# Up products of the MLP and FFN loops as one 512-column product per weight tile, on an input rescaled once by GpSimd

## The reference, cut to what matters

```python
h = rmsnorm(x, norm_mlp_pre)               # first block
u = jnp.square(jax.nn.relu(h @ w_up))
x = x + rmsnorm(u @ w_down, norm_mlp_post)

# second block, layers a and b: h = rmsnorm(x, ffn_norm); up = h @ ffn_w_up  (2 x 2816 wide)
# causal 3-tap convolution over tokens with bias, silu of one half times the other, @ ffn_w_down
```

## Time and profile before

| | |
|---|---|
| median of 3 runs | 1091.08 us |
| profiled execution | 1091.15 us, span 1089.2 us |
| PE (TensorE matmul) busy | 1081.0 us, 99% of the span |
| DVE busy | 773.9 us, 71% |
| ACT busy | 641.3 us, 59% |
| POOL busy | 21.5 us, 2% |
| DMA | 183.90 MB, mean 169 GB/s |
| TensorE clock granted | 1.00 over the whole span |

### The profile page before, as it was taken

One profiled execution on the slowest core, in us unless ns is written; L12 is line 12 of the kernel. 1 busy time (PEld: TensorE's weight loads), 2 busy tenths in 40 slices (PEclk: granted clock), 3 DMA queues, 4 the chain that ended last, 5 costly groups with the idle time before them and its releaser, 6 DMA issues.

```text
span 1089.2 us, 19347 instructions
## 1 busy us (share of the span) xinstructions
PE 1081.0 (99%) x7132; PEld 946.2 (87%) x7132; DVE 773.9 (71%) x1389; ACT 641.3 (59%) x1104; POOL 21.5 (2%) x47
## 2 busy tenths in 40 slices
PE   9999999999999999999999999999999999999998
PEld 8977899998988887888888999999877789999997
DVE  5877765555567767666755877878876757787876
ACT  5477665445566657566566655555766756555553
POOL 0000000000000000000010000000001010000000
PEclk9999999999999999999999999999999999999999
DMA  8642456555646563365524565565563435656562
GB/s 314 184 143 98 147 183 200 187 184 184 194 125 211 165 197 114 101 196 187 163 72 154 164 205 187 161 211 179 169 193 103 150 116 170 198 173 211 170 197 97
DMA packets 117038, 183.90 MB, mean 169 GB/s; under 512 B 6640, under 2 KB 70384, under 8 KB 116720
## 3 DMA queue, kind: packets, MB, share of 16 engines
q1 hardware_dynamic: 116688, 182.77, 52.7%
q10 hardware_dynamic: 288, 0.29, 0.1%
HBM read 181.99 MB, written 1.05 MB: 168 GB/s over the span
## 4 chain that ended last, share of the span: by engine, by line
PE 89%; DVE 6%; ACT 3%; issue 1%; DMA 1%; SPq 0%; DVEq 0%; ACTq 0%
PE ps L687 11%; PE ps L689 10%; PE ps L688 10%; PE ps L715 9%; PE ps L717 9%; PE ps L716 9%; PE ps L777 5%; PE ps L776 5%; PE ps L778 5%; DVE w_lo L1857 3%; PE ps L878 2%; PE ps L855 1%; PE ps L908 1%; PE ps L951 1%; DVE hid L2363 1%; ACT w_hi L1263 1%
## 5 line engine op out<-in xcount | busy, mean ns | idle before, releaser
L1857 DVE TENSOR_TENSOR w_lo<-w_stage,w_hi 128x1024 fp32r<-128x1024 f32 x336 | 403.8, 1222 | 169.9 <-ACT w_hi L1263 169.0
L1263 ACT ACTIVATE w_hi<-w_stage 128x1024 fp32r<-128x1024 f32 x336 | 349.5, 1054 | 175.8 <-PE ps L689 81.7
L715 PE MATMUL ps<-aT_hi,w_hi 128*128 128x256 f32 x992 | 281.8, 284 | 0.6 <-issue 0.4
L716 PE MATMUL ps<-aT_lo,w_hi 128*128 128x256 f32 x992 | 281.1, 283 | 0.0
L717 PE MATMUL ps<-aT_hi,w_lo 128*128 128x256 f32 x992 | 281.1, 283 | 0.0
L687 PE MATMUL ps<-w_hi,aT_hi 128*128 128x512 f32 x480 | 192.8, 402 | 1.4 <-DVE w_lo L1932 0.9
L715 PEld LDWEIGHTS ps<-aT_hi,w_hi 128*128 128x128 f32 x992 | 190.5, 192 | 2.3 <-DVE w_lo L1857 0.7
L716 PEld LDWEIGHTS ps<-aT_lo,w_hi 128*128 128x128 f32 x992 | 190.5, 192 | 1.0
L717 PEld LDWEIGHTS ps<-aT_hi,w_lo 128*128 128x128 f32 x992 | 190.5, 192 | 0.0
L689 PE MATMUL ps<-w_hi,aT_lo 128*128 128x512 f32 x480 | 187.7, 391 | 0.0
L688 PE MATMUL ps<-w_lo,aT_hi 128*128 128x512 f32 x480 | 187.2, 390 | 0.0
(11 more groups left out here) (248 smaller groups left out, 1112.0 us busy)
## 6 DMA issues: line engine op xcount, KB each, us to landing
w_stage<-in_ffn_w_up SPq DMA_DIRECT2D x88, 512.0 KB, 4.7
w_stage<-in_a_w_qkv SPq DMA_DIRECT2D x72, 512.0 KB, 4.3
w_stage<-in_ffn_w_down SPq DMA_DIRECT2D x44, 512.0 KB, 3.5
w_stage<-in_w_up SPq DMA_DIRECT2D x32, 512.0 KB, 3.9
w_stage<-in_w_down SPq DMA_DIRECT2D x32, 512.0 KB, 4.3
w_stage<-in_w_in SPq DMA_DIRECT2D x24, 512.0 KB, 4.6
w_stage<-in_b_w_qkv SPq DMA_DIRECT2D x24, 512.0 KB, 4.0
w_stage<-in_w_out SPq DMA_DIRECT2D x8, 512.0 KB, 3.5
```

Of the source, the lines that this page charges most:

```text
L715: pe.matmul(o, wh, aT_hi[:, k, :], start=(k == 0), stop=False)
L716: pe.matmul(o, wh, aT_lo[:, k, :], start=False, stop=False)
L1263: act.activation(w_hi[:, slot, :], w_in[:, slot, :], ACT.Copy).then_inc(hi_done[slot], 1)
L1857: dve.tensor_tensor(w_lo[:, slot, :], w_in[:, slot, :], w_hi[:, slot, :].bitcast(F32), ALU.subtract).then_inc(lo_done[slot], 1)
```

## The change

In the MLP loop, the FFN loops and the FFN tails, the product of `w_hi` with `aT_hi` and that of `w_hi` with `aT_lo` become one product of 512 columns, whose halves go to the two halves of the PSUM bank. The third product (`w_lo` with the high part, 256 columns) adds into the first half. DVE adds the halves (`tensor_reduce` over two). As the scale can't be applied in that reduction, the input for these stages is scaled first: in each head GpSimd forms (hi + lo) times `rbc` for each of the 8 input tiles into one of two buffers (`pts`), ACT rounds it into `oT_hi` (`whole_hi`), GpSimd subtracts for `oT_lo`. TensorE waits for all 8 before the loop. The heads themselves keep the old products and scaling. In the MLP loop, relu and square become one DVE instruction (max(h, 0)·h), and ACT no longer squares.

```diff
-        oT_hi = sb("oT_hi", [P, KT, S], F32R)
-        oT_lo = sb("oT_lo", [P, KT, S], F32R)
+        oT_both = sb("oT_both", [P, 2, KT, S], F32R)
+        oT_hi, oT_lo = oT_both[:, 0], oT_both[:, 1]
...
@@ dense_cols
+                            if joined:
+                                both = ps[:, bank(stg, names[f]), :].rearrange("p (c s) -> p c s", c=2)
+                                if k == 0:
+                                    pe.matmul(both, wh, oT_both[:, :, k, :], start=True, stop=False)
+                                last = pe.matmul(o, wl, oT_hi[:, k, :], start=False, stop=False, skip_group_check=True)
+                                if k > 0:
+                                    last = pe.matmul(both, wh, oT_both[:, :, k, :], start=False, stop=(k == KT - 1))
...
@@ TensorE, MLP (each FFN likewise, both halves of its loop and its tail joined)
             down(S_, 0, 8, range(4), True, hidden_tiles(S_, 1, 0))
+            pe.wait_ge(s["whole_lo"], at(S_, "whole_lo", KT))
             S_ = st["mlp_loop"]
             with trips(pe, S_) as i:
-                dense_cols(S_, i, 0, A4)
+                dense_cols(S_, i, 0, A4, joined=True)
                 down(S_, i, 4, range(4), ready=hidden_tiles(S_, -3, i))
...
@@ ACT
+            def whole_hi(stg, ks):
+                for k in ks:
+                    act.wait_ge(s["whole"], at(stg, "whole", k + 1))
+                    act.activation(oT_hi[:, k, :], pts[:, k % 2, 0:S], ACT.Copy).then_inc(s["whole_hi"], 1)
...
             for f in range(4):
                 hidden_hi(S_, 0, f + 1, f * S)
-            square_up(S_, 0, 4, 1, B4)
+            whole_hi(S_, range(2))
+            square_up(S_, 0, 4, 1, B4, lambda pair: whole_hi(S_, range(2 + 2 * pair, 4 + 2 * pair)))
             for f in range(4):
                 split(S_, 8 + f)
                 hidden_hi(S_, 0, 4 + f + 1, f * S)
+                if f < 2:
+                    whole_hi(S_, [6 + f])
             S_ = st["mlp_loop"]
             with trips(act, S_) as i:
-                square_up(S_, i, 0, 0, A4)
+                splits(S_, range(4), i)
...
@@ ACT, FFN head
                 hidden_hi(S_, 0, 1, 0, W)
+                whole_hi(S_, range(2))
                 splits(S_, range(4, 6))
                 taps(S_, 0, B4, 1, (0, 1))
+                whole_hi(S_, range(2, 4))
                 splits(S_, range(6, 8))
                 gate(S_, 0, 2)
                 taps(S_, 0, B4, 1, (2, 3))
+                whole_hi(S_, range(4, 6))
                 splits(S_, range(8, 10))
+                whole_hi(S_, range(6, 8))
                 hidden_hi(S_, 0, 2, 0, W)
...
@@ GpSimd, once for each of the three heads
+            def whole_input(stg, scale):
+                chain.enter(stg, 0)
+                pool.wait_ge(*is_drained(scale, "scale"))
+                def low(k):
+                    pool.wait_ge(s["whole_hi"], at(stg, "whole_hi", k + 1))
+                    pool.tensor_tensor(oT_lo[:, k, :], pts[:, k % 2, 0:S], oT_hi[:, k, :].bitcast(F32),
+                                       ALU.subtract).then_inc(s["whole_lo"], 1)
+                for k in range(KT):
+                    t = pts[:, k % 2, 0:S]
+                    if k >= 2:
+                        low(k - 2)
+                        pool.wait_ge(s["whole_lo"], at(stg, "whole_lo", k - 1))
+                    chain.link(pool.tensor_tensor(t, aT_hi[:, k, :].bitcast(F32), aT_lo[:, k, :].bitcast(F32), ALU.add))
+                    pool.tensor_tensor(t, t, rbc[:], ALU.mult).then_inc(s["whole"], 1)
+                low(KT - 2)
+                low(KT - 1)
...
@@ DVE, MLP loop
+            def square_up(stg, i, n0, names):
+                for pair in range(2):
+                    split(stg, n0 + 2 * pair, i)
+                    for f in (2 * pair, 2 * pair + 1):
+                        dve.wait_ge(*is_full(stg, names[f], i))
+                        dve.tensor_reduce(hid[:, f, :], ps[:, 4 + f, :].rearrange("p (c s) -> p s c", c=2), AX.X, ALU.add)\
+                            .then_inc(drained[4 + f], 1)
+                        dve.wait_ge(*is_drained(stg, names[f], i))
+                        dve.wait_ge(s["uhi"], at(stg, "uhi", f - 3, i))
+                        dve.scalar_tensor_tensor(out=u32[:, f * S:(f + 1) * S], in0=hid[:, f, :], scalar=0.0,
+                                                 in1=hid[:, f, :], op0=ALU.max, op1=ALU.mult).then_inc(s["u"], 1)
+                    split(stg, n0 + 2 * pair + 1, i)
...
@@ DVE, FFN loops and tails: scale_up becomes
+                def join_up(stg, i, names, fs):
+                    for f in fs:
+                        dve.wait_ge(*is_full(stg, names[f], i))
+                        dve.tensor_reduce(scaled[:, f, :], ps[:, 4 + f, :].rearrange("p (c s) -> p s c", c=2), AX.X, ALU.add)\
+                            .then_inc(drained[4 + f], 1)
```

More of the change, by code:

```diff
@@ L281, in make_plan @@
     acc = [(f"acc{b}", b) for b in range(4)]
+    whole = {"pool_step": 8, "whole": 8, "whole_hi": 8, "whole_lo": 8}
     def ffn(tag):
@@ L288, in ffn @@
                   quarters=up_quarters("a", BY_DEPTH) + up_quarters("b") + [None] * 2,
-                  counts={k: 2 * v for k, v in up.items()}),
+                  counts={**{k: 2 * v for k, v in up.items()}, **whole}),
             Stage(f"ffn_{tag}_loop", trips=(U2 - 3) // 2, uses=up_names("a") + up_names("b"),
@@ L305, in make_plan @@
         Stage("mlp_head", uses=up_names("a") + up_names("b"),
-              quarters=up_quarters("a") + up_quarters("b") + [None] * 4, counts={k: 2 * v for k, v in mlp_up.items()}),
+              quarters=up_quarters("a") + up_quarters("b") + [None] * 4,
+              counts={**{k: 2 * v for k, v in mlp_up.items()}, **whole}),
         Stage("mlp_loop", trips=U1 - 2, uses=up_names("a"), quarters=up_quarters("a") + [None] * 4, counts=mlp_up),
@@ L445, in blocks_kernel @@
             "orstd", "osq", "hms", "dm", "ovar", "sig", "sq", "ms8", "rs8", "silu", "u", "uhi", "ulo", "msq", "pms", "prstd", "x_new",
-            "lam", "zeroed", "const_ready", "gate_w", "unit", "rd", "rdb", "bc", "ohi", "olo")}
+            "lam", "pool_step", "whole", "whole_hi", "whole_lo", "zeroed", "const_ready", "gate_w", "unit", "rd", "rdb", "bc", "ohi", "olo")}
         def is_full(stg, name, i=0):
@@ L697, in dense_rows, with dense_cols @@
                         after[q]()
-            def dense_cols(stg, i, n0, names, turned=None, after=None, order=BY_PAIRS, each=None):
+            def dense_cols(stg, i, n0, names, turned=None, after=None, order=BY_PAIRS, each=None,
+                           joined=False):
                 for q, (pair, deep) in enumerate(order):
@@ L714, in dense_cols @@
                                 pe.wait_ge(*is_free(stg, names[f], i))
-                            pe.matmul(o, wh, aT_hi[:, k, :], start=(k == 0), stop=False)
-                            pe.matmul(o, wh, aT_lo[:, k, :], start=False, stop=False)
-                            last = pe.matmul(o, wl, aT_hi[:, k, :], start=False, stop=(k == KT - 1))
+                            if joined:
[5 more added lines that the diff above has]
+                                    last = pe.matmul(both, wh, oT_both[:, :, k, :], start=False, stop=(k == KT - 1))
+                            else:
+                                pe.matmul(o, wh, aT_hi[:, k, :], start=(k == 0), stop=False)
+                                pe.matmul(o, wh, aT_lo[:, k, :], start=False, stop=False)
+                                last = pe.matmul(o, wl, aT_hi[:, k, :], start=False, stop=(k == KT - 1))
                             if k == KT - 1:
@@ L1198, in ffn @@
                 down(S_, 0, 8, range(2), first=True)
+                pe.wait_ge(s["whole_lo"], at(S_, "whole_lo", KT))
                 S_ = st[f"ffn_{tag}_loop"]
                 with trips(pe, S_) as i:
-                    dense_cols(S_, i, 0, A4)
+                    dense_cols(S_, i, 0, A4, joined=True)
                     await_hidden(S_, 0, i)
                     down(S_, i, 4, range(2))
-                    dense_cols(S_, i, 6, B4)
+                    dense_cols(S_, i, 6, B4, joined=True)
                     await_hidden(S_, 1, i)
@@ L1207, in ffn @@
                 S_ = st[f"ffn_{tag}_tail"]
-                dense_cols(S_, 0, 0, A4)
+                dense_cols(S_, 0, 0, A4, joined=True)
                 await_hidden(S_, 0, 0)
@@ L1572, in _, with square_up @@
             norm_rstd(nrm, 1)
-            def square_up(stg, i, n0, n, names):
+            def whole_hi(stg, ks):
+                for k in ks:
+                    act.wait_ge(s["whole"], at(stg, "whole", k + 1))
+                    act.activation(oT_hi[:, k, :], pts[:, k % 2, 0:S], ACT.Copy).then_inc(s["whole_hi"], 1)
+            def square_up(stg, i, n0, n, names, behind):
                 for pair in range(2):
@@ L1583, in square_up @@
                     split(stg, n0 + 2 * pair + 1, i)
+                    behind(pair)
```

(13 more changed lines are left out.)

4 lines of the change are left out of this document (2 added, 2 removed).

## The result

The changed kernel takes 1134.46 us, the kernel before 1091.09 us: a ratio of 1.0397 (95% interval 1.0385 to 1.0409). That is 43 us slower, where 26 were forecast, and outside the stated range. The profiled execution took 1133.55 us, its span is 1131.8 us, 42.6 more than before.

A forecast was written before the change was run, and what follows sets the result against it. TensorE, busy 99% at full clock, was taken as the bound: 1091.15 - 9.9 (products) + 30 (FFN heads) + 4.5 (MLP head) + 1.8 (tails) = 1117.5 us. Its own range was 1107 to 1125, stretched by rivals to 1094 to 1128.

The forecast's parts named there:

- What decides: Heads: TensorE waits for GpSimd's low parts before each loop, +30 us in two FFN heads, +4.5 in the MLP's.
- rival 1: Heads: no GpSimd/DVE exclusion that matters, waits 6.4 us in each FFN, none in the MLP; 1096 us, chance 0.20.
- The clock: Behind the waits: clock taken to stay at 2.4 GHz, 0 us in the sum; upper bound 33 us.
- Rival 2: Behind the same waits the clock falls and the loop's first quarter slows: +8.3 us, 1126 us, chance 0.17.
- The FFN loops: FFN loop halves: DVE busy 13.4 us plus 1.1 stays under the new 16.55, so no cost.
- The tails: FFN tails: longer DVE chain delays the last down by 0.9 us a tail, +1.8 us for both.
- The gain: Joined passes: one product in three goes, 12.9 ns for each of 768 pairs, -9.9 us; bounds 0 and 30.
- Rival 3: Joined passes: weight loading spaces products, a pair falls to 0.321 us, gain 30 us; 1076 us, chance 0.07.
- Rival 4: Joined passes: two-part input costs as much as the joined product saves, no gain; 1127.4 us, chance 0.06.
- a DVE bound: FFN loops: if a reduction cost 1250 ns, DVE would bound each half by some 0.3 us, 5 us in all.

The follow-up runs named there:

- The kernel with the waits alone: Changed kernel with the old three products and old scaling; the scaled input is made and waited for but not used: 1133.13 us, ratio 1.0388.
- The program that measured the port by itself: Separate short program, not the kernel: GpSimd multiplications alone and beside single kinds of DVE instruction; one execution, 85.46 us.
- the dummy products: Changed kernel with small dummy products on TensorE in the three waits (24 in the MLP head, 50 in each FFN head): 1128.07 us, ratio 1.0342.
- the other order on ACT: Changed kernel without the scaled input and its waits; in the FFN loops ACT rounds its second weight quarter before its first two taps: 1084.39 us, ratio 0.9938.

## Why the prediction was right and wrong

- **What decides** (right). The wait for GpSimd was forecast at 15, 15 and 4.5 us; 14.05, 14.05 and 5.66 came (5.66 + 0.1 by borders). The inside of the sum holds too: from the first copy to the last low part 23.6 us were forecast for layer b, and 22.5 came. The kernel with the waits alone gives 1133 us, nearly the whole result. The program that measured the port by itself confirms the mechanism, a whole instruction blocked, two SBUF inputs only; rival 1, waits of 6 us, is refuted.
- **The clock** (failed: put at nothing). "The nearest row says 0 and I leave it out of the sum." The nearest row was a wait of 0.9 us (the longest of before, by the list of waits, is 1.1) for one of 15, no bound at all. The trace after shows 0.50 behind each wait and 6.8 us in sum, and the dummy products give 6.4 back. The Trainium skill's rule (TensorE: Matmul & The Clock Gate, Part 1: the clock falls when TensorE idles) agrees with this trace, with 0.50 in the window from 967 to 969. Rival 2 priced it at 8.3 us; had it been the forecast, 1126 would still have been over 8 too low.
- **The FFN loops** (failed: put at nothing). "1.1 more leaves it under the new 16.55": busy time was compared with the period. In the changed kernel DVE is busy 14.2 us of a half, which fits, but between its instructions lie 3.0 us more, 2.1 of them waits for ACT (1.76 and 0.33), which in turn waits for DVE: the chain takes 17.15 us. The trace of before had this wait already (DVE, one half of layer a):

```profile
745.08 0.78 DVE L2355 TENSOR_TENSOR o_sb<-ps,o_sb 128x256 f32<-128x256 f32 x2
747.82 1.22 DVE L1857 TENSOR_TENSOR w_lo<-w_stage,w_hi 128x1024 fp32r<-128x1024 f32 x1 [1.97 <-ACT w_hi L1263]
...
752.15 0.75 DVE L2355 TENSOR_TENSOR o_sb<-ps,o_sb 128x256 f32<-128x256 f32 x2
753.49 2.14 DVE L2363 SCALAR_TENSOR_TENSOR hid<-o_sb,cols,hid 128x255 f32<-128x255 f32 x4 [0.59 <-ACT hid L1680]
```

  From the first scaling to the next weight split were 2.74 us before and are 3.04 now, from the second pair to the taps 1.34 and 1.61. So the reductions lengthen the chain by 0.57 us, not by 4 x 0.26, and before it took about 17.15 - 0.57 = 16.6 us (estimate): 0.4 under the old half of 16.98, and only just under the new one of 16.65. Hence no wait of TensorE before. The slack that was quoted, 7 us for `u_lo`, was that of one consumer; it was the splits that came late. The loops lost 5.3 us in the changed kernel, 7.0 without the head start that the waits give. The size of the reduction was right: 682 ns, where 690 were forecast.
- **The tails** (mis-sized: 3.1 for 1.8). Same cause: DVE reached the tail late. With the other order on ACT in the loops the waits fall to 0.3 us, and the last down of layer a is late by 0.47 us, half of the 0.9 forecast. So the two parts of this miss had opposite signs.
- **The gain** (mis-sized: 7.8 for 9.9). Of 12.9 ns a pair 10.2 were gained (0.325 us / 32). "Both kinds of product lie on one line" was no support, since two points always do; that the split into columns and a rest came nearly true was not known beforehand. Reading distances between starts in place of durations was right. Rival 3 (0.32 us a pair) is refuted: 0.350.
- **Rival 4** (no gain from products): refuted, as a pass is shorter by 0.33 us wherever DVE keeps up.
- **The range** ended at 1128 because the failed terms had been given no upper end of their own in it: a DVE bound was priced at 5 us and left out of the cases, and the clock's 8.3 was added to nothing else. Clock (6.8), loops (5.3) and tails (1.3 more than forecast) together made 13.4 us over the sum, the smaller gain 2.1. The range's ends also don't follow from its own words: the products' gain and waits of 22 to 43 us give 1103 to 1124, not 1107 to 1125. That changes nothing here.

## What to carry to other kernels

- A queue that waits for another is a chain: to see whether it can take more work, add its waits on the partner to its busy time and compare that with the period. If the sum comes near it, move the partner's instruction ahead (here one line in ACT's queue was worth 9 us between profiled executions) before cutting work.
- Work given to GpSimd because it is idle runs at the pace that DVE's two-input instructions leave it; where TensorE is 99% busy, as here, each wait of 5.7 us and more was paid in full and again in the clock.
- A transformation that needs a rescaled input may be had by scaling behind the product: 1085.7 us in place of 1134.5, and 5.4 us under the kernel before.

## What the runs showed of the hardware

- Two-input instructions of DVE (128x1024, SBUF) and GpSimd (128x256, SBUF) pass one for one at 1.63 us a pair (alone 1.12 and 0.69). With DVE reading PSUM neither feels the other: GpSimd took 0.69 us beside reductions (0.68 each) and 0.67 beside products of PSUM with SBUF (0.42 each).
- Waits of TensorE of 5.7 to 14 us were followed by a clock of 0.50, and cost 1.8 to 2.8 us each in the next pass. With dummy fp32 products of 128 columns in the waits, 0.22 to 0.24 us each, the next pass ran at 1.00. A wait of 2.2 us ahead of these dummies, which came four times in two runs, was followed once by 1.00 and three times by 0.50 to 0.64 over some 2 us.
- A pair of a 512- and a 256-column product costs 0.350 us, 2.6 ns more than unbroken rows of each kind (0.2271 and 0.1200 us a product), also with the 512 columns read in one piece.
- A reduction of two PSUM parts of 256 columns, 1 KB apart, took 682 ns (128x512 to 128x256).
